# Gate and up biases of a mixture of experts: split during the opening mixer, laid in 24 rows per PSUM bank, added by four matmuls of 32-row tiles

## What is computed

```python
logits = (xt @ w_router + b_router).astype(jnp.float32)
top_vals, top_idx = lax.top_k(logits, TOP_K)          # 4 of 32
top_gates = jax.nn.softmax(top_vals, axis=-1)
...
gate = xb @ w_gate[e] + b_gate[e]                     # 1024 -> 1024
up = xb @ w_up[e] + b_up[e]
gate = jnp.minimum(gate, SWIGLU_LIMIT)
up = jnp.clip(up, -SWIGLU_LIMIT, SWIGLU_LIMIT)
glu = gate * jax.nn.sigmoid(SWIGLU_ALPHA * gate)
return (glu * (up + 1.0)) @ w_down[e] + b_down[e]
```

## Time and profile before

| | us |
|---|---|
| median of 3 runs | 1851.01 (1849.62 to 1851.53) |
| the profiled execution, its own time | 1850.49 |
| its span, first to last instruction | 1849.2 |
| PE busy | 1795.0 (97%) |
| DVE busy | 1423.2 (77%) |
| ACT busy | 1179.4 (64%) |
| POOL busy | 196.3 (11%) |

### The profile page before, as it was taken

How to read it: one execution, slowest core, us unless ns; L and a number is a source line. 1 busy time by engine, 2 the same in 40 slices (tenths; PEclk the granted TensorE clock), 3 DMA queues, 4 the chain that set the end, 5 groups by cost and what they waited for, 6 DMA issues and landing times.

```text
span 1849.2 us, 20839 instructions
## 1 busy us (share of the span) xinstructions
PE 1795.0 (97%) x8267; PEld 1437.5 (78%) x8267; DVE 1423.2 (77%) x1233; ACT 1179.4 (64%) x887; POOL 196.3 (11%) x127
## 2 busy tenths in 40 slices
PE   7999969999999999999999999999999999999998
PEld 5777748888888888888888888888884777778887
DVE  4476679999999999999999999999895524665343
ACT  4353467777777777777777777777773345655232
POOL 1311010111211211111121111112001000000000
PEclk9999979999999999999999999999998999999999
DMA  7311349999999999999999999999996311122221
GB/s 261 114 46 69 132 166 352 374 364 362 370 378 365 357 380 358 369 367 372 356 364 375 365 364 368 369 366 363 375 362 250 136 69 69 46 72 94 91 77 49
DMA packets 95475, 487.16 MB, mean 263 GB/s; under 512 B 13880, under 2 KB 15456, under 8 KB 45456
## 3 DMA queue, kind: packets, MB, share of 16 engines
q1 hardware_dynamic: 81552, 462.64, 66.4%
q0 software_dynamic: 9520, 17.13, 2.5%
q10 hardware_dynamic: 4304, 6.03, 1.0%
HBM read 481.56 MB, written 20.97 MB: 272 GB/s over the span
## 4 chain that ended last, share of the span: by engine, by line
PE 92%; DVE 3%; DMA 2%; ACT 2%; issue 1%; SPq 0%; POOLq 0%; DVEq 0%; ACTq 0%
PE PS L448 85%; PE PS L683 3%; PE PS L856 1%; PE PS L868 1%; PE PS L849 1%; DVE WL L1246 1%; DMA yk<-yd 1%; DMA ring<-in_w_in_dram 1%; ACT WH L921 0%; PE PS L480 0%; DMA xg<-h2d,tok 0%; PE PS L558 0%; DMA yd<-ys,dst 0%; PE PS L888 0%; DVE sT L1364 0%
## 5 line engine op out<-in xcount | busy, mean ns | idle before, releaser
L1246 DVE TENSOR_TENSOR WL<-ring,WH 128x2048 fp32r<-128x2048 f32 x428 | 967.4, 2287 | 233.3 <-ACT WH L921 229.6
L921 ACT ACTIVATE WH<-ring 128x2048 fp32r<-128x2048 f32 x428 | 816.0, 1914 | 352.0 <-PE PS L448 345.1
L448 PE MATMUL PS<-WH,xh 128*128 128x512 f32 x1024 | 329.3, 403 | 4.2 <-ACT xh L1069 2.2
L448 PE MATMUL PS<-WL,xh 128*128 128x512 f32 x1024 | 318.0, 392 | 0.0
L448 PE MATMUL PS<-WH,xl 128*128 128x512 f32 x1024 | 274.9, 390 | 0.0
L448 PEld LDWEIGHTS PS<-WL,xh 128*128 128x128 f32 x1024 | 193.1, 189 | 41.4
L448 PEld LDWEIGHTS PS<-WH,xl 128*128 128x128 f32 x1024 | 192.8, 188 | 41.4
L448 PEld LDWEIGHTS PS<-WH,xh 128*128 128x128 f32 x1024 | 188.5, 189 | 43.5 <-ACT xh L1069 2.8
L1822 POOL DMA_INDIRECT yd<-ys,dst x32 | 74.3, 2322 | 971.2 <-ACT ys L1084 971.2
L448 PE MATMUL PS<-WH,hh 128*128 128x512 f32 x512 | 160.6, 395 | 1.1 <-ACT hh L1069 1.1
L448 PE MATMUL PS<-WL,hh 128*128 128x512 f32 x512 | 158.3, 390 | 0.0
(11 more groups left out here) (347 smaller groups left out, 2145.9 us busy)
## 6 DMA issues: line engine op xcount, KB each, us to landing
ring<-in_w_gate_dram SPq DMA_DIRECT2D x128, 1024.0 KB, 7.6
ring<-in_w_up_dram SPq DMA_DIRECT2D x128, 1024.0 KB, 7.3
ring<-in_w_down_dram SPq DMA_DIRECT2D x128, 1024.0 KB, 8.5
ring<-in_w_in_dram SPq DMA_DIRECT2D x32, 1024.0 KB, 5.2
ring<-in_w_out_dram SPq DMA_DIRECT2D x8, 1024.0 KB, 5.0
yk<-yd SPq DMA_DIRECT2D x4, 1024.0 KB, 9.5
X<-in_x_dram SPq DMA_DIRECT2D x4, 512.0 KB, 9.9
h2d<-HV ACTq DMA_DIRECT2D x4, 512.0 KB, 3.1
```

Source lines behind the costliest of these rows:

```text
L448: return P.matmul(ps, a, b, start=start, stop=stop)
L921: A.activation(WH[buf[n]], ring[spot[n]], ACT.Copy).then_inc(s_hi, 1)
L1246: V.tensor_tensor(WL[buf[n]], ring[spot[n]], WH[buf[n]].bitcast(F32), SUB).then_inc(s_lo, 1)
```

## The change

The bias parts are made in the mixer, by DVE alone, on a layout of 128 partitions (expert, quarter row) by 256: five small instructions in `vector_mixer`. POOL's queue loads the biases, stores the six parts to DRAM (`b3d`), and loads them again after the mixer's scores as four blocks of 24 rows (8 experts by 3 parts), one for each PSUM bank, at partitions 0, 32, 64 and 96. Each block holds the 32 experts as four groups of eight along its free axis. In `tensor_gate_up` four matmuls of 24 rows, each on its own 32-row tile and its own bank, stand together after p = 3; those of the up banks open their accumulation. The `sel96` column becomes one of eight columns of `sel8`.

Beside this: `M16` and `DV16` are reduced once over all four token groups and straight to float16; ACT makes two more high parts before `xh`; DVE makes no instruction between `tok` and the landing of expert 0's rows (`V.wait_ge(s_xg[0], 16)`), and counts, weights and spreads later; `scalar_gate(0)` waits for `s_sp`. The branch for experts with over 128 rows gets four times as many bias matmuls; it is not taken with these inputs.

```diff
@@ tensor_gate_up
-            if kc == 3:
-                P.wait_ge(s_bh, 3)
-                for hf in range(2):
-                    last = mm(PS[:, 2 * which + hf, :], sel96[:, e:e + 1].broadcast_to([96, 128]), b3[:, which, 512 * hf:512 * hf + 512], False, True)
+            if p == 3:
+
+                if e:
+                    P.wait_ge(s_eu, e)
+                else:
+                    P.wait_ge(s_bh, 160)
+                    P.wait_ge(s_cnt, 1)
+                for n in range(4):
+                    rows = slice(32 * n, 32 * n + 24)
+                    last = mm(PS[:, n, :], sel8[rows, e % 8:e % 8 + 1].broadcast_to([24, 128]), b3[rows, e // 8], n >= 2, n < 2)
...
@@ scalar_routing, scalar_experts
-        A.wait_ge(s_bst, 48)
-        A.activation(b3[0:32], bst, ACT.Copy).then_inc(s_bh, 1)
...
-        scalar_turn8(0, xh)
-        A.wait_ge(s_b3, 1)
-        A.activation(b3[32:64], r1, ACT.Copy)
-        A.activation(bmid, r1, ACT.Copy).then_inc(s_bh, 1)
-        A.wait_ge(s_b3, 2)
-        A.activation(b3[64:96], bst, ACT.Copy).then_inc(s_bh, 1)
-        A.wait_ge(s_bh, 3)
         A.wait_ge(s_h2, 64)
         high(first + NX - 1)
+        scalar_turn8(0, xh)
...
@@ vector_mixer
+        V.wait_ge(s_bst, 32)
+        V.tensor_copy(bp[:, 0], bst).then_inc(dv.sem, dv.one())
+        V.wait_ge(dv.sem, dv.n)
+        V.tensor_tensor(r1, bst, bp[:, 0], SUB).then_inc(dv.sem, dv.one())
...
+        V.tensor_copy(bp[:, 2], bst).then_inc(s_b3, 1)
...
@@ vector_experts
-        V.wait_ge(s_bh, 1)
-        V.tensor_tensor(r1, bst, b3[0:32], SUB).then_inc(s_b3, 1)
+        V.wait_ge(s_xg[0], 16)
         low(first + 2)
         vector_turn8(0, xh, xl)
         for q in range(1, NI):
             vector_one_hot(q)
+        low(first + 3)
+        vector_further_count()
...
@@ gpsimd_mixer, gpsimd_routing
+        G.wait_ge(s_b3, 1)
+        for w in range(2):
+            for i in range(3):
+                G.dma_start(b3d[w, :, 8 * i:8 * i + 8].rearrange("g r (q w) -> g (r q) w", q=4), bp[:, i, w]).then_inc(s_bh, 16)
...
+        G.wait_ge(s_sc, 4)
+        G.wait_ge(s_bh, 96)
+        for n in range(4):
+            G.dma_start(b3[32 * n:32 * n + 24], b3d[n // 2, :, :, 512 * (n % 2):512 * (n % 2) + 512].rearrange("g r f -> r g f")).then_inc(s_bh, 16)
```

More of the change, by code:

```diff
@@ L91, in program @@
     GtT = place("GtT", [32, 4, 128], F32)
-    sel96 = place("sel96", [96, 32], BF16)
+    sel8 = place("sel8", [128, 8], BF16)
     FC = place("FC", [128, 40], F32)
@@ L175, in routing @@
         return place(name, shape, dt, row[0] - size)
-    LG, DV, M, Gt = (routing(n, [128, 4, E], F32) for n in ("LG", "DV", "M", "Gt"))
+    LG, Gt = (routing(n, [128, 4, E], F32) for n in ("LG", "Gt"))
     M16 = routing("M16", [128, 4, E], F16)
@@ L183, in program @@
     e2 = reg("e2", [128, 4, E, K], F32, 24)
[L184 to L187, removed]
+    b3 = reg("b3", [128, 4, 512], BF16, 44)
+    bst = place("bst", [128, 2, 256], F32, B3 + 2 * KB)
+    r1 = place("r1", [128, 2, 256], F32, B3 + 4 * KB)
+    bp = place("bp", [128, 3, 2, 256], BF16, B3 + 6 * KB)
     xg = [reg(f"xg{i}", [128, D], F32, 4 * i) for i in range(2)]
@@ L709, in rows_by_columns @@
                 for hf in range(2):
-                    mm(PS[:, b0 + hf, :], hi[:, kk], w[:, k, 512 * hf:512 * hf + 512], kk == 0 and w is wh, False)
+                    mm(PS[:, b0 + hf, :], hi[:, kk], w[:, k, 512 * hf:512 * hf + 512], kk == 0 and w is wh and b0 != 2, False)
         if turned:
@@ L715, in rows_by_columns @@
             for hf in range(2):
-                last = mm(PS[:, b0 + hf, :], lo[:, kk], wh[:, k, 512 * hf:512 * hf + 512], False, kk == 7 and b0 == 4)
+                last = mm(PS[:, b0 + hf, :], lo[:, kk], wh[:, k, 512 * hf:512 * hf + 512], False, kk == 7 and b0 != 0)
         return last
@@ L722, in tensor_gate_up @@
             which, kc = p // 4, p % 4
-            if kc == 0:
+            if p == 0:
                 if e == 0:
-                    P.wait_ge((s_lg, s_cnt)[which], (2, 1)[which])
+                    P.wait_ge(s_lg, 2)
                     P.wait_ge(s_x1, 8)
                 else:
-                    P.wait_ge((s_eg, s_eu)[which], e)
+                    P.wait_ge(s_eg, e)
             last = rows_by_columns(n_g[e] + p, kc, 2 * which, xh, xl, 0 if p else t_rows[e] + 1)
-            if kc == 3:
-                P.wait_ge(s_bh, 3)
-                for hf in range(2):
-                    last = mm(PS[:, 2 * which + hf, :], sel96[:, e:e + 1].broadcast_to([96, 128]), b3[:, which, 512 * hf:512 * hf + 512], False, True)
+            if p == 3:
[7 more added lines that the diff above has]
+                    last = mm(PS[:, n, :], sel8[rows, e % 8:e % 8 + 1].broadcast_to([24, 128]), b3[rows, e // 8], n >= 2, n < 2)
             last.then_inc(s_mm, 1)
@@ L1075, in scalar_gate @@
             A.wait_ge(s_eh, e)
+        else:
+            A.wait_ge(s_sp, 1)
         A.activation(eg, PS[:, 0:2, :], ACT.Relu, scale=-1.0, bias=C[:, LIM:LIM + 1]).then_inc(ac.sem, ac.one())
@@ L1281, in vector_mixer @@
         low(ahead(n_v))
-        for i in range(3):
-            V.tensor_copy(sel96[32 * i:32 * i + 32], C[0:32, IDENT:IDENT + 32])
+        with nc.allow_low_precision(reason="zeros and ones"):
+            V.tensor_reduce(sel8, ident.rearrange("p (g r) -> p r g", r=8), AX, ADD)
         low(ahead(n_v + 1))
+        V.wait_ge(s_bst, 32)
+        V.tensor_copy(bp[:, 0], bst).then_inc(dv.sem, dv.one())
+        V.wait_ge(dv.sem, dv.n)
+        V.tensor_tensor(r1, bst, bp[:, 0], SUB).then_inc(dv.sem, dv.one())
+        V.wait_ge(dv.sem, dv.n)
+        V.tensor_copy(bp[:, 1], r1).then_inc(dv.sem, dv.one())
+        V.wait_ge(dv.sem, dv.n)
+        V.tensor_tensor(bst, r1, bp[:, 1], SUB).then_inc(dv.sem, dv.one())
+        V.wait_ge(dv.sem, dv.n)
+        V.tensor_copy(bp[:, 2], bst).then_inc(s_b3, 1)
         V.wait_ge(s_fr, 1)
@@ L1452, in choices @@
                             mf[:, a:b, 0:K].unsqueeze(2).broadcast_to([128, n, E, K]), ALU.is_equal).then_inc(dv.sem, dv.one())
[L1453 to L1463, removed]
         choices(0, 3, 1)
         choices(3, 4, 2)
+        V.wait_ge(dv.sem, dv.n)
+        with nc.allow_low_precision(reason="zeros and ones"):
+            V.tensor_reduce(M16, eq, AX, ADD).then_inc(s_m16, 1)
+        V.tensor_tensor(e2, eq, C[:, TOKK:TOKK + 16].rearrange("p (j k) -> p j k", j=4).unsqueeze(2).broadcast_to([128, 4, E, K]),
+                        MUL).then_inc(dv.sem, dv.one())
+        V.wait_ge(dv.sem, dv.n)
+        with nc.allow_low_precision(reason="whole numbers to 2048"):
+            V.tensor_reduce(DV16, e2, AX, ADD)
+        V.wait_ge(s_m16, 1)
         V.wait_ge(s_pos, 1)
-        V.scalar_tensor_tensor(P1, PS[:, 3, 0:128].rearrange("p (j e) -> p j e", j=4), 1.0, M, ADD, MUL)
+        V.scalar_tensor_tensor(P1, PS[:, 3, 0:128].rearrange("p (j e) -> p j e", j=4), 1.0, M16, ADD, MUL)
         V.tensor_copy(cnt, PS[:, 3, 128:160]).then_inc(s_cnt, 1)
@@ L1519, in vector_experts @@
     def vector_experts():
+        V.wait_ge(s_xg[0], 16)
+        low(first + 2)
+        vector_turn8(0, xh, xl)
+        for q in range(1, NI):
+            vector_one_hot(q)
+        low(first + 3)
         vector_further_count()
@@ L1524, in vector_experts @@
         V.tensor_tensor(GK, GK, sm.unsqueeze(2).broadcast_to([128, 4, 4]), MUL).then_inc(s_gk, 1)
-        V.wait_ge(s_bh, 1)
-        V.tensor_tensor(r1, bst, b3[0:32], SUB).then_inc(s_b3, 1)
[L1527 to L1530, removed]
         V.wait_ge(s_gk, 1)
         spread_out(Gt, GK).then_inc(s_sp, 1)
-        V.wait_ge(s_bh, 2)
-        V.tensor_tensor(bst, r1, bmid, SUB).then_inc(s_b3, 1)
         low(first + NX - 1)
@@ L1776, in gpsimd_mixer @@
         G.dma_start(brc, b_router[0].partition_broadcast(128)).then_inc(s_small, 16)
+        for w, b in enumerate((b_gate, b_up)):
+            G.dma_start(bst[:, w], b[0].rearrange("e (q w) -> (e q) w", q=4)).then_inc(s_bst, 16)
         G.wait_ge(s_c, 16)
@@ L1857, in program @@
     whole -= 1
-    NL = 8
+    NL = 10
     def further_lists():
@@ L1878, in further_lists @@
         V.tensor_reduce(ofs[:, 0:NV], mt, AX, ADD).then_inc(s_lists, 1)
+        V.memset(wide8, 0.0).then_inc(s_lists, 1)
+        V.wait_ge(s_lists, 9)
+        for g in range(4):
+            last = V.tensor_copy(wide8[:, g, 8 * g:8 * g + 8], sel8)
+        last.then_inc(s_lists, 1)
         V.wait_ge(s_lists, NL)
@@ L1934, in further_tensor @@
         for n in range(4):
-            last = mm(PS[:, n, :], sc.broadcast_to([96, 128]), b3[:, n // 2, 512 * (n % 2):512 * (n % 2) + 512], True, False)
+            rows = slice(32 * n, 32 * n + 24)
+            for g in range(4):
+                last = mm(PS[:, n, :], sc[rows, g:g + 1].broadcast_to([24, 128]), b3[rows, g], g == 0, False)
         last.then_inc(s_step, 1)
```

16 lines of the change are left out of this document (9 added, 7 removed).

## The result

| | before | after |
|---|---|---|
| median | 1850.6 us (6 runs, 1847.8 to 1851.53) | 1859.14 us (6 runs, 1857.8 to 1859.63) |
| span of the profiled execution | 1849.2 us | 1858.1 us |

The ratio is 1.0046, interval 1.0034 to 1.0057. The changed kernel is 8.5 us slower. The forecast was 1833 us with a range of 1823 to 1845; the result lies above it.

A forecast was written before the change was run, and what follows sets the result against it. PE's stream of large matmuls was taken to bound the kernel. Savings of 3.3 us before the first expert matmul, 4.4 in expert 0 and 9.9 from biases made 17.6 off 1850.5: 1833 us, range 1823 to 1845.

The forecast's parts named there:

- Every 512-column matmul costs that, bias or weight: PE's expert matmuls: each 512-column one costs 0.2275 us, so the old four biases cost 0.91 us per expert.
- gather: POOL's gather of expert 0's rows, with DVE kept idle: 0.99 us instead of 2.95, 1.96 us won.
- expert 0 with its biases: PE in expert 0: 4.4 us won from a removed wait and half-pace matmuls, and 0.3 for its biases.
- group of biases: Four bias matmuls per expert on four row tiles: 0.60 us instead of 0.91, saving 0.31 per expert, 9.9 in all.
- Distance of the tiles: Within the bias group: row-tile matmuls start 0.03 us apart; tile shape changes cost 0.09 going in and 0.19 coming out.
- The start: DVE's routing chain between mixer and experts: `tok` comes 1.3 us earlier, at about 235.9, and the gather with it.
- The 2.29 us that the prediction counted as won: DVE's instructions between the two `choices`, from 230.36 to 232.65, which the change removes.
- What was given no price: Mixer's bias split, some 2.5 us of DVE, and POOL's six stores, 0.6 to 0.8 us each: hidden in idle time.
- The tiles do run together: Bias group; the rival claimed row tiles do not run together: group 1.19 us, 1851.8 in all, no change; chance 0.08.
- the shape does cost: Bias group; the rival claimed tiles together with shape changes free: group 0.32 us, 1824 in all; chance 0.17.
- the other engines do not bind: Steady experts; the rival claimed DVE or DMA holds an expert at 35.8 us: 1843 in all; chance 0.08.
- The slower rival: Bias group; tiles run one after the other with bare weight loads: group 1.58 us, 1864 in all; chance 0.07.

The follow-up runs named there:

- experiment 1: The changed kernel with 32 unused bytes behind `sel8`, so tiles behind it lie where the kernel before has them: 1832.62 us, ratio 0.9898 to the kernel before.
- Experiments 2 and 3: The kernel before with only unused bytes added: behind `sel96`, 32 gave 1877.18 us and 64 gave 1872.33 us; 32 ahead of `WH0` gave 1851.24 us.
- experiment 6: The kernel of experiment 1 with a separate `xh` for each expert, at 32 offsets from 0 to 1,504 bytes: 1843.2 us in a single execution.
- 9: The kernel of experiment 1 without DVE's wait for the landing of expert 0's rows ahead of the low part of first + 2: 1837.13 us, ratio 0.9925.
- 10: The kernel of experiment 1 with ACT's high parts of first + 3 and first + 4 put back behind `xh`: 1832.03 us, ratio 0.99.
- the control of 5: The kernel of experiment 1 with `xh` alone moved to 48 KB of R0, without the extra 32 bytes: 1834.48 us, ratio 0.9909.
- Experiment 5: The kernel of experiment 1 with `xh` alone moved to 48 KB plus 32 bytes of R0: 1843.29 us, ratio 0.9961.

## Why the prediction was wrong

**The step that failed** is the smallest part of the change: "The `sel96` column becomes one of eight columns of `sel8`". It was given no price, because only the instruction on it was looked at and not the 32 bytes that it gives back. The assumption beneath it was "Every 512-column matmul costs that, bias or weight": 0.2275 us is the cost at one distance between the operands, 0.231 to 0.234 at most others. In place of 9.6 us won in experts 1 to 31, 4.8 were lost, and the second block, for which no change was forecast, lost 9.6.

The term missing from the sum is worth 26.5 us by the medians (after less experiment 1). Experiments 2 and 3 show it with no other edit present. In the profiled executions the difference is 0.6 us up to the first expert matmul, 1.5 in expert 0, 14.1 in experts 1 to 31 and 9.4 in the second block, together 25.6, which is all of the difference of the spans (1858.1 - 1832.5). The last two, 23.5 us, are the term's. The 0.6 us can't be told from what the mixer varies. The 1.5 us in expert 0 are mostly something else, the clock: in the kernel after it was granted at 0.50 (1.2 GHz) from 248.6 to 251.6 us, in which 11 matmuls ran, in experiment 1 at 0.96 from 248.0 to 251.0, with 17. In experiment 6, where `xh` of expert 0 is aligned, expert 0 took 26.1 us with such a late clock, against 26.3 after and 24.8 in experiment 1.

**The rest of the sum held.** With the bytes back the profiled execution is 16.7 us shorter than before, where 17.6 were forecast, and 1832.62 us stand against 1833:

| step | forecast | experiment 1 |
|---|---|---|
| first expert matmul | 244.5, 3.3 us earlier | 245.06, 2.7 earlier |
| gather | 0.99 us | 1.14 us |
| expert 0 with its biases | 4.7 us shorter | 4.9 (24.77 us, before 29.64) |
| group of biases | 0.60 us | 0.57 by leaving it out |
| an expert | 35.5 us | 35.48 us |
| second block | no change | 0.2 us longer |

That the total comes within 0.4 us is in part luck. Expert 0 had the full clock early in this execution: it took 24.8 us, and 25.0 to 26.1 in the traces of experiments 6, 9, 10 and the control of 5. And two errors in the price of the group cancel in part.

- **Distance of the tiles.** 0.03 us was taken, 0.003 to 0.004 is true, and the changes of shape cost more than the 0.28 us allowed for them. The two errors cancel in part. From 567.58 to 569.49 in experiment 1 pass six weight matmuls (1.36 us) and a group, which leaves 0.55; less the stream of 0.2275 about 0.3 us is for the two changes of shape. The piece behind a group also starts its matmuls 0.23 us apart, which makes 0.57.
- **The start.** `tok` came 0.9 us later than I said (236.81). The first routing instruction began 0.7 us late behind the mixer, at 228.87 us, inside the 225.7 to 229.1 of the other traces. From the first read of logits to `tok` pass 7.94 us, 8.97 before: 1.0 us won of the 1.3. The three wide instructions were as forecast. What is missing is a small DVE conversion that ran into POOL's clearing of `xg`. The timeline of DVE and of POOL in the kernel after:

```profile
231.76 0.79 DVE L1462 CAST mf<-mi 128x8 f32<-128x8 uint32 x1
...
232.91 0.69 DVE L1471 TENSOR_REDUCE M<-eq 128x128 f16<-128x512 f32 x1
...
234.23 0.69 DVE L1476 TENSOR_REDUCE DV<-e 128x128 f16<-128x512 f32 x1
...
236.81 0.15 DVE L1509 TENSOR_SCALAR tok<-dst 128x1 int32<-128x1 int32 x1
...
230.68 1.84 POOL L1847 MEMSET xg<- 128x1024 f32 x2 [48.86 <-PE PS L452]
```

  The conversion has 0.79 us where the one of three groups at 230.26 has 0.18; it ends with the clearing (232.52). The kernel before had the same loss, in one of the five instructions that were taken out:

```profile
230.95 0.93 DVE L1456 CAST M<-M 128x96 f16<-128x96 f32 x1
...
229.97 1.84 POOL L1828 MEMSET xg<- 128x1024 f32 x2 [76.92 <-PE PS L448]
```

  It ended with the clearing too (231.81). The 2.29 us that the prediction counted as won held that wait, and the wait did not go with the instructions; it moved to the next one that met the clearing.
- **What was given no price**, the split in the mixer and POOL's stores, stayed hidden as far as the traces can tell: the first logits are read at 225.7 to 229.1 us with the split and at 226.0 to 229.0 without it.
- **The rivals.** The tiles do run together, the shape does cost, and the other engines do not bind: an expert without biases passes in 34.91 us. The slower rival named bare weight loads and gave 1864. The result is near that number and has nothing to do with that cause; a group in it costs 0.57 us, not 1.15 or more.

**What stays open.** Which reads meet, and why 192 is milder than the others, no run tells. Experiment 5 points to the next stationary operand and not the one in use, but no run has set one against the other, nor does one tell why the distance stays long for two to five matmuls after the bad pair. In pieces behind a break in the stream, starts stand 0.224 to 0.240 us apart at the good distance too.

## What to carry to other kernels

Where matmuls in a stream bound a kernel, read the distance between their starts for each buffer, before and after a change: a step from 0.227 to 0.234 us shows in no wait and in no busy share, and was worth 1.4% here. Where tiles are placed one after the other, an edit that resizes one moves all behind it. For streams like this one (float32, 512 columns, a weight load for each) keep the distance between stationary and moving operands at a multiple of 256 bytes by padding; other types and shapes were not tried. Check the padding first when untouched code gets slower. For the few microseconds of a gather that everything waits for, keep DVE from long subtractions, and keep large transfers from being released ahead of its rows.

## What was not expected of the hardware

- A matmul with 512 float32 columns started every 0.227 us with its operands 0 modulo 256 bytes apart, every 0.229 to 0.230 us at 192, and every 0.231 to 0.234 us at the other multiples of 32 tried.
- Four 24-row matmuls on four row tiles started 3 to 4 ns apart, each with a weight load of 91 ns of its own; on one row tile they stood 0.215 us apart.
- A gather took 1.14 us of POOL with DVE idle, and 2.22 us when a 2.28 us subtraction of DVE ran into it. Its rows landed 3.2 us after the instruction's end, and 5.0 us after it when a 1 MB weight piece had been issued in between.
